# Block-Toeplitz rows of the S5 layer: eight shifted matmuls against eight copies within SBUF

## The chip, the cores and the metric

The kernel runs on one core of a Trainium2 chip, in float32 throughout (some matmuls on operands split into two fp32r parts). The metric is the device time of one launch, in microseconds.

## The reference, cut to what matters

Two blocks of two layers each are applied to x of 512 tokens by 1024 channels. The change touches the first layer of the first block alone, in its state-space half: an S5 layer with 32 groups of 16 channels, each group with 64 complex states.

```python
bu_re = jnp.einsum('blgp,gnp->blgn', ug, bb_re)
bu_im = jnp.einsum('blgp,gnp->blgn', ug, bb_im)
_, _, x_re, x_im = lax.associative_scan(_complex_affine_combine, (a_seq_re, a_seq_im, bu_re, bu_im), axis=1)
y = jnp.einsum('blgn,gpn->blgp', x_re, c_re) - jnp.einsum('blgn,gpn->blgp', x_im, c_im)
```

Everything else (the mLSTM half of that layer, two gated feed-forward parts, an HGRN2 layer, two attention layers with spatial gating and two convolved feed-forward parts) is computed by code that the diff leaves alone.

## The kernel before, in words

Each engine has its own hand-written program (`@block.sync`, `gpsimd`, `tensor`, `scalar`, `vector`), which runs in the order written; semaphores are the only links. Weights come in slabs of 128 by 1024 numbers through a ring of four: SyncE loads `w_raw`, ScalarE copies it to `w_hi` (L1336, `split`), VectorE subtracts to get `w_lo` (L1849), TensorE multiplies each slab in three terms (`product`, L673, 24 matmuls of 512 columns per slab).

The first layer begins with `project()`: twelve slabs of the input projection, with the preparation of the S5 layer laid between them. The sequence of 512 steps is cut into 64 blocks of STEP = 8. For each group g the kernel needs three 128 by 128 matrices: `s5_in` (8 inputs of 16 channels to the 128 state rows), `s5_out` (state rows to 8 outputs of 16 channels), and `s5_conv`, the block-Toeplitz matrix that maps the 8 inputs of a block directly to its 8 outputs. Row block k of a column block j of `s5_conv` is the kernel matrix for a lag, and is zero where the lag is negative. All lags of all groups stand once in `s5_k` (128 partitions, 32 groups by 16 columns, a view of the tile `sq_sum`): TensorE computes it in line 851 (32 small matmuls, 64 passes), ScalarE copies it from PSUM in line 1434. `s5_conv[:, :, j]` is `s5_k` shifted down by 16·(7 − j) partitions. Before the change this shift is a matmul with a shifted identity (`shifted`, L859, eight of them, one for each j), into PSUM banks 5 to 7 in turn, and ScalarE copies each bank to SBUF (L1449). TensorE does this between the last two pairs of slabs; ScalarE between `gate_in(1)` and `gate_in(2)`.

In the meantime VectorE runs a long list of its own: the powers for `s5_q` and `s5_out`, a wait for ScalarE (L2112), cosine and sine tables by doubling (L2125 to L2153), two `w_lo` slabs, a few small operations on `lb_raw` with an exponential by ScalarE in their middle (L1454). GpSimd issues the DMAs that store `us` to DRAM (L619) and load it again by step into `u_step` (L624, eight DMAs of 128 KB); it waits next for the result `ys_step` (L625).

`s5_core()` follows on TensorE. `enter(i)` (L871, 16 passes each) forms the states' inputs for 8 groups; ScalarE copies them to `s5_state` (L1471, behind the exponential of L1454 on its queue); `swap_inputs(i)` (L878) exchanges halves; VectorE turns and scans (`turn_and_sum`, L2184). When all four quarters are scanned, TensorE does `swap_sums` (L882), VectorE `turn_back`, and TensorE `leave(i)`: for each of 32 groups one matmul with `s5_conv[:, g]` as the stationary operand on 64 columns of `u_step` (L889), and one with `s5_out[:, g]` on 63 columns of the state (L891). An fp32 matmul shows as two passes in the profile, each with a weight load of 128 columns. ScalarE copies the outputs (L1475), GpSimd stores and reloads them (L628 to L631), and TensorE goes on with `lstm_front()` (L914 and after).

Of the kernel before, what the change touches and what calls it, by code (L numbers as in the profile page):

```python
# [18 lines left out]
ACT = mybir.ActivationFunctionType  # L19
AX = mybir.AxisListType  # L20

P = 128
# [36 lines left out]
STEP = 8  # L59
# [92 lines left out]
def program(nc, a):  # L152
    ctx = ExitStack()
    with ctx:
# [11 lines left out]
        def sem(name):  # L166
            return ctx.enter_context(nc.semaphore(name))
# [64 lines left out]
        s5_out = m("s5_out", [P, GROUPS, STEP, GW], 40)  # L232
        s5_conv = m("s5_conv", [P, GROUPS, STEP, GW], 56)
        s5_cos = m("s5_cos", [P, GROUPS, CH], 72)
# [6 lines left out]
        s5_cx = m("s5_cx", [P, GROUPS, GW], 84)  # L241
        s5_k = sq_sum[:].rearrange("p (g w) -> p g w", g=GROUPS)
        s5_flat = tmp[:, 2:4].rearrange("p t n -> p (t n)")
# [123 lines left out]

        prep, hgrn = signals("prep"), signals("hgrn")
        s5 = {k: sem(f"s5_{k}") for k in ("pe_to_vector", "pe_to_scalar", "vector_to_pe", "scalar_to_pe")}

# [196 lines left out]
        def _(pool):  # L567
# [54 lines left out]
            for i in range(STEP):  # L622
                k = STEP - 1 - i
                pool.dma_start(u_step[GW * k:GW * k + GW], by_step[i]).then_inc(us_loaded, 16)  # L624
            pool.wait_ge(ys_ready, 1)  # L625
            by_step = ys_dram.rearrange("(g p) j c -> j p g c", p=GW)
# [23 lines left out]
        def _(pe):  # L650
# [173 lines left out]
            def project():  # L824
# [29 lines left out]
                product(h_hi, h_lo, [KD], 2)  # L854
                pe.wait_ge(prep["scalar_to_pe"], n(prep["scalar_to_pe"]))
                for j in range(STEP):
                    out = take(5 + j % 3)
                    off = P - GW * (STEP - 1 - j)
                    nc.tensor.matmul(out[:], shifted[:, off:off + P], s5_k.rearrange("p g w -> p (g w)"),  # L859
                                     start=True, stop=True).then_inc(prep["pe_to_scalar"], 1)  # L860
                product(h_hi, h_lo, [KD], 2)

            def s5_core():
# [20 lines left out]
                def leave(i):  # L884
                    out = take(i)
                    pe.wait_ge(s5["vector_to_pe"], n(s5["vector_to_pe"]))
                    for g in range(8):
                        c = g * CH
                        nc.tensor.matmul(out[:, c:c + CH], s5_conv[:, 8 * i + g].rearrange("p j w -> p (j w)"),  # L889
                                         u_step[:, 8 * i + g], start=True, stop=False)  # L890
                        mm = nc.tensor.matmul(out[:, c + 1:c + CH], s5_out[:, 8 * i + g].rearrange("p j w -> p (j w)"),  # L891
                                              s5_state[:, 8 * i + g, 0:CH - 1], start=False, stop=True)
                    mm.then_inc(s5["pe_to_scalar"], 1)

                pe.wait_ge(us_loaded, 16 * STEP)
                enter(0)
                enter(1)
# [429 lines left out]
        def _(act):  # L1327
# [74 lines left out]
            def project():  # L1402
# [26 lines left out]
                for i in range(GROUPS // 4):  # L1429
# [4 lines left out]
                nc.scalar.activation(s5_k, bank[4][:].rearrange("p (g w) -> p g w", g=GROUPS), ACT.Copy)\  # L1434
                    .then_inc(prep["scalar_to_pe"], 1)
                act.drain().then_inc(bank_free[4], 1)
# [8 lines left out]
                for t in (0, 1):  # L1445
                    gate_in(t)
                for j in range(STEP):
                    act.wait_ge(prep["pe_to_scalar"], n(prep["pe_to_scalar"]))
                    nc.scalar.activation(s5_conv[:, :, j], bank[5 + j % 3][:].rearrange("p (g w) -> p g w", g=GROUPS),  # L1449
                                         ACT.Copy).then_inc(bank_free[5 + j % 3], 1)  # L1450
                for t in (2, 3):
# [1442 lines left out]
```

## Time and profile before

| | us |
|---|---|
| median of 3 runs | 2513.64 (2512.18 to 2513.93) |
| the profiled execution | 2510.49 |
| its span, first to last instruction | 2508.7 |

| engine | busy us | share of the span |
|---|---|---|
| TensorE matmul | 2397.1 | 96% |
| TensorE weight load | 1948.0 | 78% |
| VectorE | 1478.1 | 59% |
| ScalarE | 1078.2 | 43% |
| GpSimd | 160.4 | 6% |

The span is what the profiler sees; 1.8 us of the execution lie around it. TensorE's matmuls are pipelined, so that successive ones overlap in the records: the distance from one start to the next tells the cost, and the sum of the durations is larger. The granted clock is given as a share of full speed: 1.00 is 2.4 GHz, 0.50 is 1.2 GHz. All that the change touches lies in the first 175 us of the span.

### The profile page before, as it was taken

What the parts mean: (1) busy time and instruction counts of PE and PEld (TensorE: products, weight loads), DVE (VectorE), ACT (ScalarE), POOL (GpSimd) and SP (SyncE); (2) the same over time, 40 slices, a digit from 0 to 9 for tenths busy, and PEclk for the clock granted to TensorE, in tenths of its full rate; (3) what the DMA queues carried; (4) which work ended last, traced back from release to release, by engine and by line L of the source; (5) the groups of instructions that cost most, each with busy time, mean ns of one, the idle gap of its engine ahead of it and who ended that gap; (6) DMA issues with size and microseconds to landing.
All of it is one profiled execution on the core that took longest, in us unless ns stands there. A gap on an engine that the chain in (4) does not pass through costs nothing.

```text
span 2508.7 us, 33052 instructions
## 1 busy us (share of the span) xinstructions
PE 2397.1 (96%) x11563; PEld 1948.0 (78%) x11563; DVE 1478.1 (59%) x2157; ACT 1078.2 (43%) x1454; POOL 160.4 (6%) x159
## 2 busy tenths in 40 slices
PE   8987999999989999999999999999999989999999
PEld 6755788888778877888887667788888767788887
DVE  7985464442567745545324776887633686687732
ACT  5344543332456544333324562545422473454421
POOL 2010200000100001000002021000011011000000
PEclk9998999999999999999999999999999999999999
DMA  7320233333222222333333202333333201233331
GB/s 171 84 62 23 76 109 100 92 92 97 71 76 75 75 64 71 103 97 90 100 96 99 68 1 68 99 102 92 94 98 102 84 24 51 84 100 100 88 100 63
DMA packets 400950, 209.65 MB, mean 84 GB/s; under 512 B 18131, under 2 KB 397655, under 8 KB 400871
## 3 DMA queue, kind: packets, MB, share of 16 engines
q1 hardware_dynamic: 397111, 199.65, 27.8%
q0 software_dynamic: 3424, 8.91, 1.4%
q8 instruction: 49, 0.80, 0.1%
q14 instruction: 30, 0.25, 0.0%
q10 hardware_dynamic: 336, 0.05, 0.0%
HBM read 204.38 MB, written 4.19 MB: 83 GB/s over the span
## 4 chain that ended last, share of the span: by engine, by line
PE 84%; DVE 9%; ACT 3%; issue 2%; DVEq 1%; DMA 0%; ACTq 0%; SPq 0%
PE bank L673 66%; PE bank L709 4%; PE bank L1262 2%; PE bank L713 2%; DVE w_lo L1849 1%; DVEq L1878 1%; DVE small L2645 1%; PE bank L988 1%; ACT w_hi L1336 1%; PE bank L1238 1%; DVE tmp L1881 1%; PE bank L1213 1%; PE bank L1134 0%; PE bank L739 0%; PE bank L1092 0%
## 5 line engine op out<-in xcount | busy, mean ns | idle before, releaser
L1849 DVE TENSOR_TENSOR w_lo<-w_raw,w_hi 128x1024 fp32r<-128x1024 f32 x380 | 475.0, 1251 | 630.4 <-ACT w_hi L1336 625.4
L673 PE MATMUL bank<-h_hi,w_hi 128*128 128x512 f32 x1840 | 727.2, 395 | 4.2 <-DVEq L1878 3.9
L673 PE MATMUL bank<-h_lo,w_hi 128*128 128x512 f32 x1840 | 717.5, 390 | 0.0
L673 PE MATMUL bank<-h_hi,w_lo 128*128 128x512 f32 x1840 | 717.3, 390 | 0.0
L1336 ACT ACTIVATE w_hi<-w_raw 128x1024 fp32r<-128x1024 f32 x380 | 401.6, 1058 | 668.4 <-PE bank L673 651.3
L673 PEld LDWEIGHTS bank<-h_hi,w_hi 128*128 128x128 f32 x1840 | 346.5, 188 | 79.8 <-issue 8.1
L673 PEld LDWEIGHTS bank<-h_hi,w_lo 128*128 128x128 f32 x1840 | 346.5, 188 | 73.3 <-issue 2.9
L673 PEld LDWEIGHTS bank<-h_lo,w_hi 128*128 128x128 f32 x1840 | 346.1, 188 | 73.3
L673 PE MATMUL bank<-hid_hi,w_hi 128*128 128x512 f32 x704 | 273.9, 389 | 0.0
L673 PE MATMUL bank<-hid_hi,w_lo 128*128 128x512 f32 x704 | 273.9, 389 | 0.0
L673 PE MATMUL bank<-hid_lo,w_hi 128*128 128x512 f32 x704 | 273.9, 389 | 0.0
L673 PEld LDWEIGHTS bank<-hid_hi,w_lo 128*128 128x128 f32 x704 | 132.2, 188 | 27.6
L673 PEld LDWEIGHTS bank<-hid_hi,w_hi 128*128 128x128 f32 x704 | 132.2, 188 | 27.4
L673 PEld LDWEIGHTS bank<-hid_lo,w_hi 128*128 128x128 f32 x704 | 132.2, 188 | 27.2
L1336 ACT ACT_TABLE_LOAD x44 | 56.5, 1283 | 120.6 <-PE bank L673 120.2
L1790 ACT ACTIVATE tmp<-bank,par 128x512 f32<-128x512 f32 x88 | 68.0, 772 | 85.4 <-DVE bank L2797 85.4
L1881 DVE TENSOR_TENSOR tmp<-tmp 128x512 f32<-128x512 f32 (+3 forms) x122 | 75.0, 623 | 26.7 <-DVE tmp L1881 13.5
L709 PE MATMUL bank<-h_hi,w_hi 128*128 128x512 f32 x168 | 71.5, 425 | 16.0 <-ACT h_hi L1597 9.9
L2797 DVE TENSOR_TENSOR bank<-bank,sq_sum 128x512 f32<-128x512 f32 x88 | 61.6, 700 | 31.8 <-PE bank L673 16.3
L2804 DVE SCALAR_TENSOR_TENSOR tmp<-bank,par,tmp 128x511 f32<-128x511 f32 x88 | 66.0, 750 | 12.0 <-DVE tmp L1890 3.1
L709 PE MATMUL bank<-h_hi,w_lo 128*128 128x512 f32 x168 | 69.7, 415 | 0.0
L1890 DVE SCALAR_TENSOR_TENSOR tmp<-bank,par,tmp 128x511 f32<-128x511 f32 x88 | 65.8, 747 | 2.8 <-ACT tmp L1790 2.3
(462 smaller groups left out, 2856.2 us busy)
## 6 DMA issues: line engine op xcount, KB each, us to landing
w_raw<-in_ffn_w SPq DMA_DIRECT2D x120, 512.0 KB, 3.8
w_raw<-in_w_up SPq DMA_DIRECT2D x88, 512.0 KB, 3.8
w_raw<-in_c_w_in SPq DMA_DIRECT2D x32, 512.0 KB, 4.1
w_raw<-in_w_down SPq DMA_DIRECT2D x32, 512.0 KB, 3.9
w_raw<-in_w_in SPq DMA_DIRECT2D x28, 512.0 KB, 3.9
w_raw<-in_w_o SPq DMA_DIRECT2D x16, 512.0 KB, 3.9
w_raw<-in_ab_w_in SPq DMA_DIRECT2D x12, 512.0 KB, 6.2
w_raw<-in_ffn_w SPq DMA_DIRECT2D x16, 384.0 KB, 3.4
```

Source lines behind the costliest of these rows:

```text
L673: mm = nc.tensor.matmul(out[:], w[:, s, k], v[:, kt], start=(kt == 0 and w is w_hi and v is hi), stop=(kt == sum(slabs) - 1 and v is lo))
L709: nc.tensor.matmul(out[:], w[:, s, k], hi[:, k], start=(first and w is w_hi), stop=False)
L713: mm = nc.tensor.matmul(out[:], w_hi[:, s, k], lo[:, k], start=False, stop=last)
L988: mm = nc.tensor.matmul(bank[b][:], w[:, b, k], v[:, k], start=(first and w is w_hi and v is h_hi), stop=(last and v is h_lo))
L1262: mm = nc.tensor.matmul(out[:], w[:, s, k0 + k], v[:, k], start=(k == 0 and w is w_hi and v is hi), stop=(k == 3 and v is lo))
L1336: nc.scalar.activation(w_hi[:, s], w_raw[:, s], ACT.Copy).then_inc(hi_done, 1)
L1790: nc.scalar.activation(tmp[:, 2 * p + v], bank[(first + 2 * p + v) % RING][:], ACT.Identity, scale=col_at("up_conv", k + 2 * KF), bias=col ...
L1849: nc.vector.tensor_tensor(w_lo[:, s], w_raw[:, s], w_hi[:, s].bitcast(F32), ALU.subtract).then_inc(lo_done, 1)
L1881: step(nc.vector.tensor_tensor(out, x0, x1, op))
L1890: step(nc.vector.scalar_tensor_tensor(out, x0, sc, x1, op0, op1))
L2797: own(nc.vector.tensor_tensor(bank[b][:], bank[b][:], inv_all, ALU.mult), bank_scaled)
L2804: ins = nc.vector.scalar_tensor_tensor(c_[:, 0:SEQ - 1], bank[b][:, 1:SEQ], col_at("up_conv", k + 4 * KF), c_[:, 0:SEQ - 1], ALU.mult, ALU ...
```

## The change

The eight shifted matmuls and their eight copies out of PSUM are taken away. `s5_k` is written with the group as its innermost index, (w g) in place of (g w), so that each partition's 512 numbers can be moved as one run. GpSimd, once it has issued the loads of `u_step`, waits for `s5_k` (`s5_k_ready`) and issues eight DMAs within SBUF: copy j moves partitions 0 to 127 − r of `sq_sum` to partitions r to 127 of `s5_conv[:, j]`, with r = 16·(7 − j). Seven memsets on GpSimd write zeros to the partitions above. `s5_conv` has the layout [P, STEP, GW, GROUPS], so that the stationary operand of a group is read with a distance of 32 numbers (128 bytes) between neighbours. TensorE waits for all eight copies and all seven memsets before `enter(0)`.

```diff
-        s5_conv = m("s5_conv", [P, GROUPS, STEP, GW], 56)
+        s5_conv = m("s5_conv", [P, STEP, GW, GROUPS], 56)
...
-        s5_k = sq_sum[:].rearrange("p (g w) -> p g w", g=GROUPS)
+        s5_k = sq_sum[:].rearrange("p (w g) -> p g w", g=GROUPS)
...
                 pool.dma_start(u_step[GW * k:GW * k + GW], by_step[i]).then_inc(us_loaded, 16)
+            pool.wait_ge(s5_k_ready, 1)
+            for j in range(STEP):
+                r = GW * (STEP - 1 - j)
+                pool.dma_start(s5_conv[r:P, j].rearrange("p w g -> p (w g)"), sq_sum[0:P - r]).then_inc(s5_conv_in, 16)
+            for j in range(STEP - 1):
+                nc.gpsimd.memset(s5_conv[0:GW * (STEP - 1 - j), j], 0.0).then_inc(s5_conv_zero, 1)
             pool.wait_ge(ys_ready, 1)
...
                 product(h_hi, h_lo, [KD], 2)
-                pe.wait_ge(prep["scalar_to_pe"], n(prep["scalar_to_pe"]))
-                for j in range(STEP):
-                    out = take(5 + j % 3)
-                    off = P - GW * (STEP - 1 - j)
-                    nc.tensor.matmul(out[:], shifted[:, off:off + P], s5_k.rearrange("p g w -> p (g w)"),
-                                     start=True, stop=True).then_inc(prep["pe_to_scalar"], 1)
                 product(h_hi, h_lo, [KD], 2)
...
-                        nc.tensor.matmul(out[:, c:c + CH], s5_conv[:, 8 * i + g].rearrange("p j w -> p (j w)"),
+                        nc.tensor.matmul(out[:, c:c + CH], s5_conv[:].rearrange("p j w g -> p (j w) g")[:, :, 8 * i + g],
                                          u_step[:, 8 * i + g], start=True, stop=False)
...
                 pe.wait_ge(us_loaded, 16 * STEP)
+                pe.wait_ge(s5_conv_in, 16 * STEP)
+                pe.wait_ge(s5_conv_zero, STEP - 1)
                 enter(0)
...
-                    .then_inc(prep["scalar_to_pe"], 1)
+                    .then_inc(s5_k_ready, 1)
...
-                for j in range(STEP):
-                    act.wait_ge(prep["pe_to_scalar"], n(prep["pe_to_scalar"]))
-                    nc.scalar.activation(s5_conv[:, :, j], bank[5 + j % 3][:].rearrange("p (g w) -> p g w", g=GROUPS),
-                                         ACT.Copy).then_inc(bank_free[5 + j % 3], 1)
```

GpSimd's queue between the loads of `u_step` and the stores of `ys_step`. Before:

```order
L624 DMA u_step<-us_dram 16x32x64 x8
L628 DMA ys_dram<-ys_step 16x32x64 x8
L629 DMA us<-us_dram 128x4x512
```

With the change (line numbers from here on are later by seven on this queue):

```order
L625 DMA u_step<-us_dram 16x32x64 x8
L629 DMA s_conv<-sq_sum 16x512
L629 DMA s_conv<-sq_sum 32x512
L629 DMA s_conv<-sq_sum 48x512
L629 DMA s_conv<-sq_sum 64x512
L629 DMA s_conv<-sq_sum 80x512
L629 DMA s_conv<-sq_sum 96x512
L629 DMA s_conv<-sq_sum 112x512
L629 DMA s_conv<-sq_sum 128x512
L631 MEMSET s_conv 112x512
L631 MEMSET s_conv 96x512
L631 MEMSET s_conv 80x512
```

Four more memsets, of 64, 48, 32 and 16 partitions, follow, and then the stores of `ys_step`: fifteen instructions stand in a place where there were none.

ScalarE's queue from the copy of `s5_k` (the tile `sq_sum`) on. Before:

```order
L1434 ACTIVATE sq_sum<-bank 128x512
L1336 ACTIVATE w_hi<-w_raw 128x1024
L1443 ACT_TABLE_LOAD
L1443 ACTIVATE zs<-bank 128x512
L1336 ACTIVATE w_hi<-w_raw 128x1024
L1443 ACTIVATE zs<-bank 128x512
L1449 ACTIVATE s_conv<-bank 128x32x16 x8
L1336 ACTIVATE w_hi<-w_raw 128x1024
```

With the change:

```order
L1437 ACTIVATE sq_sum<-bank 128x32x16
L1339 ACTIVATE w_hi<-w_raw 128x1024
L1446 ACT_TABLE_LOAD
L1446 ACTIVATE zs<-bank 128x512
L1339 ACTIVATE w_hi<-w_raw 128x1024
L1446 ACTIVATE zs<-bank 128x512
L1339 ACTIVATE w_hi<-w_raw 128x1024
```

The eight copies are gone and nothing takes their place; the order of the rest is the same, as it is on TensorE's and VectorE's queues.

## Rows read from the trace of the kernel before

**Rows 1.** Chain that ended last, 84 to 176 us: start, us, what.

```profile
110.90 1.30 DVE s_sin L1887
...
115.14 0.59 ACT s_state L1471
...
138.29 0.22 PE bank L891 x2
```

**Rows 2.** Timeline of VectorE, 84 to 136 us: start, us, instruction, [idle before <-releaser].

```profile
84.19 0.62 DVE L1881 TENSOR_TENSOR s_v<-s_v 128x32 f32<-128x32 f32 x4
...
112.22 2.36 DVE L1849 TENSOR_TENSOR w_lo<-w_raw,w_hi 128x1024 fp32r<-128x1024 f32 x2
...
115.27 0.17 DVE L1881 TENSOR_TENSOR small<-small 128x8 f32<-128x8 f32 x1 [0.33 <-ACT small L1454]
...
117.07 0.69 DVE L1881 TENSOR_TENSOR s_w<-bank,s_sin 128x512 f32<-128x512 f32 x1 [0.44 <-PE bank L878]
...
135.22 0.69 DVE L1881 TENSOR_TENSOR s_w<-bank,s_sin 128x512 f32<-128x512 f32 x1 [2.28 <-PE bank L882]
```

**Rows 3.** Timeline of TensorE's matmuls, 92 to 172 us.

```profile
93.58 7.03 PE L859 MATMUL bank<-sq_sum,lead 128*128 128x512 f32 x16
100.05 0.80 PE L673 MATMUL bank<-h_hi,w_hi 128*128 128x512 f32 x1
...
111.37 3.68 PE L871 MATMUL bank<-u_step,s_in 128*128 128x64 f32 x32
115.87 1.10 PE L878 MATMUL bank<-s_state,early 128*128 128x512 f32 x2 [0.82 <-ACT s_state L1471]
...
133.03 5.09 PE L882 MATMUL bank<-s_z,early 128*128 128x512 f32 x8 [9.82 <-DVEq L1878]
137.96 0.33 PE L889 MATMUL bank<-u_step,s_conv 128*128 128x64 f32 x2
...
152.28 3.65 PE L914 MATMUL bank<-xm,s_v 128*64 128x512 f32 x8
```

**Rows 4.** Timeline of ScalarE, 76 to 130 us.

```profile
81.01 0.60 ACT L1434 ACTIVATE sq_sum<-bank 128x512 f32<-128x512 f32 x1 [7.44 <-PE bank L851]
...
115.02 0.22 ACT L1454 ACTIVATE small<-small 128x16 f32<-128x16 f32 x1 [0.61 <-DVEq L1878]
```

**Rows 5.** Groups of weight loads: busy us, mean ns | idle before.

```profile
L889 PEld LDWEIGHTS bank<-u_step,s_conv 128*128 128x128 f32 x64 | 9.7, 192 | 0.5 <-issue 0.5
L891 PEld LDWEIGHTS bank<-s_state,s_out 128*128 128x128 f32 x64 | 9.7, 192 | 0.0
```

**Rows 6.** Groups of VectorE instructions by shape.

```profile
L2277 DVE TENSOR_TENSOR gated_ys<-ys,gate 128x512 f32<-128x512 f32 x4 | 4.4, 1105 | 3.8 <-ACTq L1518 3.8
...
L2283 DVE TENSOR_TENSOR h_lo<-gated_ys,h_hi 128x512 fp32r<-128x512 f32 x4 | 2.7, 686 | 0.3
...
L2619 DVE TENSOR_REDUCE small<-prob_t 128x8 f32<-128x512 f32 x8 | 4.9, 680 | 3.5 <-ACTq L1711 3.5
...
L2216 DVE TENSOR_REDUCE small<-tmp 128x96 f32<-128x384 f32 x1 | 0.8, 828 | 0.0
```

**Rows 7.** Stretches, of line 851 alone: PE, PEld busy (count), clock, DMA.

```profile
76.00:77.00 1.00, 1.00 (x11) 1.00 (x10) 1.00 0.30 37
79.00:80.00 1.00, 1.00 (x7) 1.00 (x6) 0.50 1.28 225
```

**Rows 8.** Stretches: PE, PEld, DVE, ACT, POOL busy (count), clock, DMA.

```profile
125.00:126.00 1.00, 0.00 (x0) 0.00 (x0) 0.90 (x2) 0.00 (x0) 0.00 (x0) 0.81 0.00 0
135.00:136.00 1.00, 1.00 (x3) 0.48 (x2) 0.79 (x2) 0.00 (x0) 0.00 (x0) 0.57 0.00 0
```

**Rows 9.** GpSimd's timeline, then DMA issues: KB each, median us to landing.

```profile
75.38 5.04 POOL L624 DMA_DIRECT2D u_step<-us_dram  x8 [4.79 <-DMA us_dram<-us]
...
u_step<-us_dram POOLq DMA_DIRECT2D x8, 128.0 KB, 5.8
```

**Rows 10.** Timeline of VectorE while GpSimd adds squares.

```profile
257.79 1.72 DVE L1849 TENSOR_TENSOR w_lo<-w_raw,w_hi 128x1024 fp32r<-128x1024 f32 x1 [0.52 <-ACT w_hi L1336]
```

More of the change, by code:

```diff
@@ L368, in program @@
         prep, hgrn = signals("prep"), signals("hgrn")
+        s5_k_ready, s5_conv_in, s5_conv_zero = (sem(k) for k in ("s5_k_ready", "s5_conv_in", "s5_conv_zero"))
         s5 = {k: sem(f"s5_{k}") for k in ("pe_to_vector", "pe_to_scalar", "vector_to_pe", "scalar_to_pe")}
```

## The prediction

> **What bounds the kernel now.** I read the chain that ended last first, in the stretch of the change. From 84 to 114.5 us it names VectorE alone, the tables of lines 2125 to 2153 and then `w_lo` [rows 1]. It passes through ScalarE's copy of the states' input at 115.14, through VectorE's scans up to 133, and from there through TensorE: `swap_sums`, then L889 and L891 in turn. So TensorE is busy at 93 us without holding anything up. The other views say the same. VectorE's timeline has no idle bracket after 84.19, where it passes its wait for ScalarE (L2112), until 115.27, where it waits 0.33 us for an exponential, and 117.07, where it waits 0.44 us for `swap_inputs(0)` [rows 2]. TensorE ends `enter(1)` at 115.05 (111.37 and 3.68) and waits until 115.87 for ScalarE; it waits 9.82 us more before L882 [rows 3]. ScalarE could not have copied the states' input earlier, because the exponential ahead of it on its queue began at 115.02 and waited for VectorE itself [rows 4]. After 133 the picture turns: TensorE runs from 137.96 to 152.28 through `leave` without a gap, and `lstm_front` begins right behind it.
>
> **What goes.** The eight shifted matmuls hold TensorE from 93.58 to 100.05, 6.47 us [rows 3]. All of it lies beside VectorE's list. Nothing in that list waits for it: the `w_hi` slabs that come 6.5 us earlier (the third at about 99.6, the fourth at 105) feed the two `w_lo` at 112.22, which VectorE reaches only then, without idling [rows 2]. TensorE ends `enter(1)` at 108.6 in place of 115.05 and waits for the same copy at 115.14. Gain: 0. ScalarE's eight copies go too; its queue had room there, gain 0. What is late next is VectorE's list, which the change doesn't shorten.
>
> **What the earlier end costs.** TensorE's pause before `swap_inputs(0)` grows from 0.82 to about 7.3 us. The pause before L882 shows what such a pause does: the matmul before it ended at 123.2 (133.03 less 9.82), the granted clock fell during 125 to 126 (mean 0.81, then 0.50), and it was still at 1.2 GHz when work came back, up to 135.9 (mean 0.57 in the slice) [rows 3, 8]. There VectorE could begin 2.19 us after the first matmul's start (135.22 against 133.03); behind L878, at 2.4 GHz, 1.20 us (117.07 against 115.87) [rows 2, 3]. I take the difference, +1.0 us (0 if the clock stays up; the two passes of L878 take 1.10 us at 2.4 GHz, so 1.1 more at most). It lands on VectorE's chain. The later quarters are covered: TensorE is done with them at 123.2, VectorE's part lasts until 133.
>
> **The copies.** GpSimd is through with `u_step` at 80.42 and `s5_k` is written at 81.61 [rows 9, 4]. Its eight issues took 5.04 us, so eight more end at about 86.7; with 5.8 us to landing (the median of the `u_step` DMAs) the last lands at about 92.5. Together they move 576 partition rows of 2 KB, 1.2 MB, somewhat more than the 1 MB of `u_step`. TensorE asks for them at about 105, and would lose nothing until 111.4, where `enter(0)` starts today. Cost 0; the cover is 12 us, and without it each microsecond beyond 111.4 is one on the path. The memsets follow the issues. GpSimd's adds of 512 columns are the nearest rows: one beside `w_lo` stretched it to 1.72 us against 1.18 (2.36 for two) [rows 10, 2]. If each of seven memsets did the same to VectorE, whose list is the path here, that would be 3.5 us; they read nothing and the instructions beside them are short, so I take 0, and keep 0 to +3.5. The Trainium skill (SBUF — State Buffer, Who interferes with whom and the two separate sides) says that a VectorE operation on two SBUF inputs is blocked only by a GpSimd operation that reads SBUF; by that rule the memsets cost nothing here.
>
> **`s5_k` written with a distance of 128 bytes.** It took 0.60 us [rows 4]; at 1.8 times (below) it ends 0.5 us later, at 82.1. VectorE asks at 84.19 and GpSimd has 12 us. Cost 0.
>
> **The stationary operand read with a distance of 128 bytes.** This is the term that decides. `leave` runs 128 passes in 14.32 us, 112 ns each [rows 3], and the loads fill that time: those of L889 and L891 have 192 ns each and 0.5 and 0.0 us idle [rows 5]. A load that takes longer is paid in full, 64 times. No row shows a weight load with a distance. The nearest rows are VectorE's with 32 bytes between neighbours. `gated_ys`, written so, takes 1105 ns, where the like operation on the same tile without it takes 686. The sum over `tmp`, read so, takes 828 ns for 384 numbers, where L2619 takes 680 for 512 in a row [rows 6]. Less some 170 ns that even 8 columns take [rows 2], that is 1.83 against 1.01 ns, and 1.71 against 1.00 ns for each number. As a factor (1.7) on 112 ns: 78 ns more, 5.0 us. As a time for each number (1.83 by 128 columns, 234 ns): 122 ns more, 7.8 us. I take half speed, 224 ns, between the two: 64 · 0.112 = +7.2 us. The lower end is 0, as TensorE is another engine. The Trainium skill speaks on both sides. SBUF — State Buffer, Door 1: The DMA port swizzle, says that SBUF is read in lines of 16 bytes and that an fp32 access is free of cost up to a distance of 4, so 32 pays; VectorE's rows agree. TensorE: Matmul & The Clock Gate, LDWEIGHTS, gives the load's time by the number of columns alone, 107 ns for 128 (the 112 ns here agree), and by that the term is 0 and the sum +1.0.
>
> **Sum.** 0 + 1.0 + 0 + 7.2 = +8.2 us. Everything after `leave` hangs on its end, `lstm_front` directly and the way of `ys_step` through DRAM too, so it arrives whole. The profiled execution would take 2518.7 in place of 2510.49; that execution is 3.15 us under the median of the runs, so I put the sum on the median: 2521.8. A measurement of this kernel can tell about 0.2%, 5.0 us, from no change.
>
> **Rivals.**
> 1. *The strided load costs nothing* (chance 0.27). The loads keep 112 ns, and the pause's +1.0 is all: 2514.6, no change. For it: the load works through columns at a pace of its own, 0.88 ns each, and no row shows TensorE slowed by a layout. Against it: rows 6. It decides at 63 ns more for each load, 175 ns: below that the change stays within 5.0 us.
> 2. *Slower loads thin the matmuls and the clock falls in `leave`* (0.12). Line 851 shows it: matmuls of 16 columns behind full weight loads; in 76 to 77 clock 1.00 and 11 passes, in 79 to 80 clock 0.50 and 7 passes [rows 7]. If `leave` fell so a quarter of the way through (I guess the place), its other 16.1 us would take 11/7 as long, 9.2 us more, and `lstm_front` would start slow, some 1.4 more (half of 133.03 to 135.9): 8.2 + 10.6 = +18.8, 2532.4. Against it: L889's matmuls have 64 columns, L851's 16.
> 3. *GpSimd or the copies come late* (0.04): memsets that block VectorE, or copies landing after 111.4; with the forecast's loads up to 2525.3.
> 4. *TensorE sets the start of the core after all* (0.04): the 6.47 us come through and the loads are free, 2507.2, faster. Rows 2 speak against it.
>
> That the change doesn't do what it says has no chance of its own: the queues show the copies in and the matmuls out, and both layouts are plain in the code.
>
> **The numbers.** The forecast has 0.53; its own range is 5.0 + 0 to 7.8 + 1.1, 2518.6 to 2522.5, and 2526 with the memsets' bound. The range takes in rival 1 with the runs' scatter of about 1 us each way, and goes part of the way to rival 2: 2512.5 to 2529. Slower 0.53 + 0.12 + 0.03 = 0.68, same 0.27 + 0.01 = 0.28, faster 0.04.
>
> **What would show it.** TensorE busy to 108.6 and then idle to about 115.9; clock 0.50 around 115.9 and VectorE's first turn at about 118.1 in place of 117.07; `leave` 21.5 us long in place of 14.3, with L889's loads about twice as long and L891's unchanged; the copies landed by 95. Wrong it would be if `leave` stayed at 14.3, if its clock fell, if TensorE stood at the copies' semaphore, or if VectorE's list from 84 to 114.5 changed in length.

## The result and the profile after

| | before | after |
|---|---|---|
| median of 4 runs, us | 2512.91 (2510.12 to 2513.93) | 2530.28 (2529.18 to 2531.36) |
| ratio, 95% interval | | 1.0070 [1.0058, 1.0082] |
| the profiled execution, us | 2510.49 | 2530.91 |
| its span, us, and mean granted clock | 2508.7, 0.979 | 2529.1, 0.970 |

The change makes the kernel slower by 17.4 us, where the forecast said 8.2: slower, as forecast, but more than twice as much, and 1.3 us above the range. Lines after the edit have moved: L851, L871, L878, L882, L889, L891 and L914 of before are L858, L872, L879, L883, L890, L892 and L917 here.

The chain that ended last shows a first loss where the forecast had none. It runs through VectorE's list as before [rows 1], but one operation of 128 by 32 numbers stands in it with 3.37 us:

```profile
89.00 3.37 DVE s_v L1884
```

VectorE's timeline gives the same operation, and then the turns of the four quarters, which stood at 117.07, 121.08, 125.10 and 129.12 before:

```profile
84.64 0.62 DVE L1880 TENSOR_TENSOR s_v<-s_v 128x32 f32<-128x32 f32 x4 [0.95 <-ACTq L1440]
...
88.91 3.44 DVE L1884 TENSOR_SCALAR s_v<-s_v 128x32 f32<-128x32 f32 x1
...
118.97 0.17 DVE L1880 TENSOR_TENSOR small<-small 128x8 f32<-128x8 f32 x1 [0.33 <-ACT small L1453]
...
121.72 0.69 DVE L1880 TENSOR_TENSOR s_w<-bank,s_sin 128x512 f32<-128x512 f32 x1 [1.38 <-PE bank L879]
...
126.84 0.69 DVE L1880 TENSOR_TENSOR s_w<-bank,s_sin 128x512 f32<-128x512 f32 x1 [1.31 <-PE bank L879]
...
131.96 0.69 DVE L1880 TENSOR_TENSOR s_w<-bank,s_sin 128x512 f32<-128x512 f32 x1 [1.30 <-PE bank L879]
...
135.98 0.69 DVE L1880 TENSOR_TENSOR s_w<-bank,s_sin 128x512 f32<-128x512 f32 x1 [0.20 <-DVE s_z L2183]
```

The reader is to see three things. VectorE waited at 84.64 for ScalarE (0.95 us, none before) and went on 0.45 us later than before (84.19). The TENSOR_SCALAR at 88.91 took 3.44 us; its like at 85.18, 85.93 and 86.68 took 0.17. So the operation behind the exponential stands at 118.97 and not at 115.27 [rows 2], 3.70 us later. And the turns are 5.12, 5.12 and 4.02 us apart where they were 4.02 each time, so that the offset grows from 4.65 at the first turn to 6.86 at the last two.

GpSimd's timeline puts its seven memsets exactly under the slow operation, 88.99 to 92.31; ScalarE's shows the strided write of `s5_k`, 1.07 us against 0.60 [rows 4]:

```profile
84.79 4.21 POOL L629 DMA_DIRECT2D s_conv<-sq_sum  x8 [4.83 <-ACT sq_sum L1437]
88.99 3.32 POOL L631 MEMSET s_conv<- 112x512 f32 x7
```

```profile
83.43 1.07 ACT L1437 ACTIVATE sq_sum<-bank 128x512 f32<-128x512 f32 x1 [10.25 <-PE bank L858]
```

Before comparing stages, one difference has to be set aside, since it lies ahead of the change. `s5_k` was copied 2.42 us later here (83.43 against 81.01), although nothing in front of it was edited: the clock fell to 0.50 during the computation of `s5_k` from about 74 us on, and before from about 78 us on. In the profiled executions of all twelve kernels that copy begins anywhere from 80.65 to 83.43. What hangs on this moment is scatter and not the change.

TensorE's timeline (start, us, instruction, [idle before <-releaser]), to be read beside rows 3:

```profile
107.33 3.68 PE L872 MATMUL bank<-u_step,s_in 128*128 128x64 f32 x32
119.57 2.04 PE L879 MATMUL bank<-s_state,early 128*128 128x512 f32 x2 [8.56 <-ACT s_state L1470]
...
139.89 6.73 PE L883 MATMUL bank<-s_z,early 128*128 128x512 f32 x8 [6.86 <-DVEq L1877]
146.46 0.43 PE L890 MATMUL bank<-u_step,s_conv 128*128 128x64 f32 x2
...
146.95 0.59 PE L890 MATMUL bank<-u_step,s_conv 128*128 128x64 f32 x2
147.38 0.39 PE L892 MATMUL bank<-s_state,s_out 128*128 128x63 f32 x2
147.60 0.59 PE L890 MATMUL bank<-u_step,s_conv 128*128 128x64 f32 x2
...
152.83 0.64 PE L890 MATMUL bank<-u_step,s_conv 128*128 128x64 f32 x2
153.27 0.64 PE L892 MATMUL bank<-s_state,s_out 128*128 128x63 f32 x2
153.69 0.64 PE L890 MATMUL bank<-u_step,s_conv 128*128 128x64 f32 x2
...
171.75 6.11 PE L917 MATMUL bank<-xm,s_v 128*64 128x512 f32 x8
177.79 3.84 PE L921 MATMUL bank<-lstm_bd,xm 128*128 128x128 f32 x32
```

`enter(1)` ended at 111.0 (107.33 and 3.68) and the pause before `swap_inputs(0)` was 8.56 us. `leave` begins at 146.46 and `lstm_front` at 171.75: 25.3 us in place of 14.32. Early in `leave` a pair of passes of L890 takes 0.43 us (146.95 to 147.38) and one of L892 0.22; late in it both take 0.43. The stretches of TensorE (busy (count), clock, DMA share, GB/s) say why the second half of that is so:

```profile
120.00:125.00 5.00, 5.00 (x19) 0.50 0.44 129
125.00:130.00 5.00, 5.00 (x19) 0.50 0.00 0
145.00:150.00 5.00, 5.00 (x26) 0.90 0.00 0
150.00:155.00 5.00, 5.00 (x30) 0.78 0.01 3
155.00:160.00 5.00, 5.00 (x25) 0.50 0.00 0
```

The clock was 0.50 from 120 to 130, at a time when TensorE worked without a gap, was mostly back in 145 to 150, and fell again during 150 to 155, though TensorE had not stood still. The mean loads of the two lines, both 192 ns in rows 5, mix both clocks:

```profile
L890 PEld LDWEIGHTS bank<-u_step,s_conv 128*128 128x128 f32 x64 | 17.2, 317 | 0.7 <-issue 0.5
L892 PEld LDWEIGHTS bank<-s_state,s_out 128*128 128x128 f32 x64 | 14.8, 284 | 0.0
```

Summed as offsets of the two profiled executions: 3.70 at the exponential, 0.95 more at the first turn, 2.21 more at the fourth, 1.64 more in the phase of L883 (6.57 us from its first start to `leave`, 4.93 before), 10.97 in `leave`, 2.46 in the first eight passes of `lstm_front` (171.75 to 177.79, 6.04 us, against 3.58). That is 21.93. Of it 1.5 is lost again further on, since the kernel before has the clock at 0.50 from 188 to 193 and the changed one at the same work does not until 211; 20.4 is left, the difference of the spans.

### The profile page after: what moved, and what is told of

Its sections match the earlier page's. It is cut to its first block, busy times and chain, and to the rows that moved or that the text cites. A ratio compares the mean times of both kernels' runs of the same rounds, so it can differ in the third digit from the quotient of the medians.

```text
span 2529.1 us, 33034 instructions
## 1 busy us (share of the span) xinstructions
PE 2413.1 (95%) x11547; PEld 1964.0 (78%) x11547; DVE 1481.5 (59%) x2157; ACT 1073.8 (42%) x1446; POOL 167.9 (7%) x174
## 4 chain that ended last, share of the span: by engine, by line
PE 86%; DVE 7%; ACT 3%; issue 2%; DVEq 1%; DMA 0%; ACTq 0%; SPq 0%
PE bank L680 67%; PE bank L716 4%; PE bank L1265 2%; PE bank L720 2%; DVE w_lo L1848 1%; DVEq L1877 1%; DVE small L2644 1%; PE bank L991 1%; ACT w_hi L1339 1%; PE bank L1241 1%; PE bank L1216 1%; PE bank L890 1%; DVE tmp L1880 1%; PE bank L1137 0%; PE bank L892 0%
```

## The experiments

The theory behind the first four: the loss has three independent parts, the strided read (with the clock in `leave`), the memsets that hold VectorE, and TensorE's pause. Each kernel was compared with the kernel before on its own chip. The offsets of the profiled executions against the profiled one of before are collected here, in us; the ratios are of all runs.

| kernel | exponential (ScalarE) | 4th turn | start of `leave` | length of `leave` | second line of `lstm_front` | ratio [95%] |
|---|---|---|---|---|---|---|
| changed | +3.70 | +6.86 | +8.50 | 25.3 | +21.93 | 1.0070 [1.0058, 1.0082] |
| e1, strided layouts alone | +2.11 | +2.10 | +2.69 | 25.7 | +15.80 | 1.0051 [1.0034, 1.0068] |
| e2, consecutive read | +3.19 | +6.34 | +7.90 | 14.3 | +7.91 | 1.0016 [1.0006, 1.0026] |
| e3, zeros by ScalarE | +2.12 | +5.28 | +6.96 | 25.3 | +20.41 | 1.0069 [1.0052, 1.0086] |
| e4, idle matmuls kept | +2.04 | +3.63 | +3.90 | 25.7 | +16.87 | 1.0068 [1.0051, 1.0085] |
| e6, zeros behind the flag | −0.31 | +2.84 | +4.42 | 25.3 | +17.83 | 1.0057 [1.0040, 1.0074] |
| e7, all three undone | 0.00 | −0.01 | +1.57 | 14.3 | +1.58 | 1.0006 [0.9994, 1.0018] |
| e8, copies in pieces | −0.17 | +0.77 | +2.31 | 14.3 | +2.32 | 1.0000 [0.9987, 1.0012] |
| e9, e6 and pause filled | −0.89 | −0.34 | −0.05 | 25.7 | +12.91 | 1.0033 [1.0019, 1.0046] |
| e10, e8 and pauses filled | +1.17 | +3.01 | +2.79 | 14.4 | +2.87 | 1.0007 [0.9996, 1.0017] |

The ratios, times 2513 us, lie up to 4.6 us under the last offsets (e4 and e7 agree with theirs): some 1.5 us is the part lost again further on, and the profiled execution of before was 2.4 us under its median. The rest is scatter; an interval is 2.5 to 4.3 us to each side, so a term of a microsecond is read from the profiles and only the large ones from the medians as well. Absolute times of different chips are not compared: the medians of the kernel before lie between 2511.36 and 2516.30 on those used here.

### e1: the strided layouts alone

```diff
 (against the kernel before)
-        s5_conv = m("s5_conv", [P, GROUPS, STEP, GW], 56)
+        s5_conv = m("s5_conv", [P, STEP, GW, GROUPS], 56)
-        s5_k = sq_sum[:].rearrange("p (g w) -> p g w", g=GROUPS)
+        s5_k = sq_sum[:].rearrange("p (w g) -> p g w", g=GROUPS)
...
-                        nc.tensor.matmul(out[:, c:c + CH], s5_conv[:, 8 * i + g].rearrange("p j w -> p (j w)"),
+                        nc.tensor.matmul(out[:, c:c + CH], s5_conv[:].rearrange("p j w g -> p (j w) g")[:, :, 8 * i + g],
```

> The kernel before with the new layouts alone: the eight shifted matmuls and ScalarE's copies stay, s5_k and s5_conv have the group innermost, so the stationary operand in leave() is read with a distance of 128 bytes. No copies by DMA, no memsets, no longer pause ahead of swap_inputs(0). Theory (the strided loads are slow by themselves, about 215 ns against 112, and make the clock fall in leave): leave() takes 21 us at first and, after some 6 us, 213 ns for each pass, 25 us in all; lstm_front starts slow; 11 to 13.5 us over the kernel before, 2524 to 2527. Rival 1 (the clock falls in leave only because of the pause before it): leave() 20.9 us at clock 1.00, 6.6 us over before, 2519.5. Rival 2 (the loads are slow only at the lower clock): no change, 2513.

Measured: 2523.67 us (2523.15 to 2524.94), 1.0051, +12.8. TensorE's timeline:

```profile
140.65 0.43 PE L889 MATMUL bank<-u_step,s_conv 128*128 128x64 f32 x2
...
166.34 5.39 PE L914 MATMUL bank<-xm,s_v 128*64 128x512 f32 x8
171.66 3.84 PE L918 MATMUL bank<-lstm_bd,xm 128*128 128x128 f32 x32
```

`leave` takes 25.7 us here too, and `lstm_front` starts slow (5.32 us to L918, against 3.58), although TensorE had no pause ahead of `swap_inputs` and VectorE's turns were 4.0 us apart. So the strided read alone lengthens `leave` by 11 us and lowers the clock in it, as the theory said (the time is 0.3 us under its range); with neither 20.9 us nor 14.3, both rivals fall. The 2.1 us at the exponential are two waits: 0.77 us for `s5_k` at 84.40, and 1.74 us for the fourth `w_hi` at 115.36. Both come from a TensorE that was late: it released `s5_k` at 83.17, 2.16 us later than before (the scatter named above), the copy of the fourth `w_hi` began 2.72 us later (114.28 against 111.56), and with the eight shifted matmuls still in TensorE's queue that lateness reached VectorE. So the eight matmuls had been off the path by about one microsecond (2.72 less 1.74).

### e2: the layouts and copies stay, the read is consecutive

```diff
-                        nc.tensor.matmul(out[:, c:c + CH], s5_conv[:].rearrange("p j w g -> p (j w) g")[:, :, 8 * i + g],
+                        nc.tensor.matmul(out[:, c:c + CH], s5_conv[:].rearrange("p j w g -> p (j w g)")[:, P * (8 * i + g):P * (8 * i + g) + P],
```

> The changed kernel, but leave() reads 128 consecutive numbers of s5_conv in place of 128 with a distance of 32, so it multiplies by numbers of the wrong places: the matrix of the state-space half is not the Toeplitz matrix, the rest is as in the changed kernel. Theory: loads of 112 ns again and leave() at 14.3 us and clock 1.00; what is left over the kernel before is the memsets' hold on VectorE (3.3), the copy of s5_k (0.5) and the clock after the pause (0.9 to 4.8): 2517 to 2521. Rival 1 (the pause makes the clock fall in leave): leave() near 25 us although the loads are consecutive, 2528 or more.

Measured: 2515.38 us (2513.04 to 2516.97), 1.0016, +4.0; less than expected.

```profile
145.86 0.33 PE L890 MATMUL bank<-u_step,s_conv 128*128 128x64 f32 x2
...
160.19 3.65 PE L917 MATMUL bank<-xm,s_v 128*64 128x512 f32 x8
```

`leave` is back at 14.33 us, so rival 1 falls, and up to its start all is as in the changed kernel but for 0.6 us. By the medians what is not the strided read costs about 4 us, then (1.5 to 6.5), and the read itself 13 to 14; by the profiles it is 7.9 and 14.0.

### e3: the zeros by ScalarE, ahead of the flag

```diff
-            for j in range(STEP - 1):
-                nc.gpsimd.memset(s5_conv[0:GW * (STEP - 1 - j), j], 0.0).then_inc(s5_conv_zero, 1)
...
                     .then_inc(s5_k_ready, 1)
+                for j in range(STEP - 1):
+                    r = GW * (STEP - 1 - j)
+                    nc.scalar.activation(s5_conv[0:r, j], lead[0:r, 0:1].unsqueeze(2).to_broadcast([r, GW, GROUPS]), ACT.Copy)\
+                        .then_inc(s5_conv_zero, 1)
```

> The changed kernel with the seven memsets moved from GpSimd to ScalarE (copies of a zero, behind the copy of s5_k, where ScalarE is idle for 6.8 us). Theory (a VectorE tensor_scalar was held for as long as GpSimd's memsets ran): the 3.44 us operation of VectorE goes back to 0.17 and the list ends 3.3 us earlier, 2527. Rival 2 (GpSimd's DMA issues or the copies themselves held VectorE): the long operation stays, now beside the issues, and the time stays at 2530. Rival 3 (ScalarE's zeros delay its next w_hi or VectorE's wait for it): up to 4 us are given back.

Measured: 2528.61 us (2527.67 to 2529.40), 1.0069. VectorE's timeline:

```profile
86.19 0.62 DVE L1882 TENSOR_TENSOR s_v<-s_v 128x32 f32<-128x32 f32 x4 [2.60 <-ACTq L1442]
86.73 0.30 DVE L1886 TENSOR_SCALAR s_v<-s_v 128x32 f32<-128x32 f32 x1
```

The slow operation is gone, but the seven copies (3.73 us) stand on ScalarE's queue ahead of the flag that VectorE waits for, and the wait of 2.60 us takes back about half of it: the exponential is 1.58 us ahead of the changed kernel's. Rival 2 falls, since GpSimd's issues are all there, and rival 3 came. The edit traded one hold for another; e6 repeats it in a better place.

### e4: eight unread matmuls where the shifted ones were

```diff
                 product(h_hi, h_lo, [KD], 2)
+                pe.wait_ge(bank_free[5], n.now(bank_free[5]) + 1)
+                for j in range(STEP):
+                    nc.tensor.matmul(bank[5][:], ident, x[:, 0], start=True, stop=True)
                 product(h_hi, h_lo, [KD], 2)
```

> The changed kernel with eight matmuls of the old size between the last two pairs of slabs, whose results nobody reads: TensorE ends enter(1) as late as before, and pauses under 4 us ahead of swap_inputs(0) (the rest of the pause is the hold on VectorE). Theory (the pause lowers the clock for the whole of s5_core): with the shorter pause swap_inputs and enter run at 2.4 GHz, VectorE's later turns no longer wait for TensorE, 2 to 5 us less than the changed kernel, 2525 to 2528; leave() still falls. Rival (3.7 us of pause are enough to lower it): no difference, 2530.

Measured: 2528.14 us (2527.99 to 2528.39), 1.0068. The pause is 2.09 us long, `swap_inputs(0)` runs at 2.4 GHz, and yet the clock falls right behind it (0.50 from 120 to 130) and the turns are 4.50, 5.12 and 4.02 apart. Here 0.5 and 1.1 us came onto VectorE's chain. VectorE's TENSOR_SCALAR was held for 2.87 us, to the end of the memsets; the TENSOR_TENSOR ahead of it overlapped the first 0.5 us of them and took its usual time. In the profile `leave` starts 4.6 us earlier than in the changed kernel, as the theory had it, but the medians (1.0068 and 1.0070) show none of that; with 4.3 us of interval to each side they don't decide.

### e5: a table of weight loads

```diff
                     mm.then_inc(out_turned, 1)
+            x_row = x[:].rearrange("p k n -> p (k n)")
...
+            for _ in range(16):
+                nc.tensor.matmul(bank[0][:, 0:64], x_row[:, 0:1017:8], x_row[:, 0:64], start=True, stop=True)
```

> The kernel before with a table of matmuls appended after its last step: for distances 1, 2, 3, 4, 5, 8, 16 and 32 between the numbers of the stationary operand, sixteen matmuls of 64 columns each; then, behind 48 matmuls of 512 columns each time, 128 thin matmuls at distance 1 and 64 at distance 32. The appended work is extra and its total time says nothing. Theory (the load is slow where neighbouring numbers lie in different 16-byte lines, and the slow loads alone lower the clock): a matmul takes about 112 ns at distances 1 to 3, 215 ns at 4 and beyond, no more at 32 than at 8; the clock falls to 1.2 GHz within the 64 strided matmuls (13.8 us at 215 ns) and stays at 2.4 GHz within the 128 consecutive ones (14.3 us at 112 ns). Rival A (it grows with the distance): times between 112 and 215 ns at 2 to 16. Rival B (the clock falls because the matmuls are thin, and distance only adds time): the 128 consecutive ones lose the clock too.

The groups of weight loads (busy us, mean ns | idle before), one line for each of the distances 1, 2, 3, 4, 5, 8, 16 and 32, each from a stretch at clock 1.00:

```profile
L1331 PEld LDWEIGHTS bank<-x 128*128 128x128 f32 x20 | 2.3, 192 | 0.0
...
L1335 PEld LDWEIGHTS bank<-x 128*128 128x128 f32 x19 | 2.3, 196 | 0.0
...
L1339 PEld LDWEIGHTS bank<-x 128*128 128x128 f32 x15 | 2.7, 260 | 0.2 <-issue 0.2
...
L1343 PEld LDWEIGHTS bank<-x 128*128 128x128 f32 x19 | 4.5, 329 | 0.0
...
L1347 PEld LDWEIGHTS bank<-x 128*128 128x128 f32 x24 | 5.4, 317 | 0.1
...
L1351 PEld LDWEIGHTS bank<-x 128*128 128x128 f32 x18 | 4.4, 334 | 0.1
...
L1355 PEld LDWEIGHTS bank<-x 128*128 128x128 f32 x22 | 4.9, 311 | 0.1
...
L1359 PEld LDWEIGHTS bank<-x 128*128 128x128 f32 x20 | 4.4, 310 | 0.0
```

A load's record grows from 192 ns (distance 1) and 196 (2) to 260 (3), 329 (4), 317 (5), 334 (8), 311 (16) and 310 (32). These records overlap; from start to start it is 110 ns a pass at distance 1 (24 us for 218, below) and 212 at 32 (6.77 us for 32). The theory held but for distance 3, where half of the rise is there already (68 of the 137 ns at distance 4), and rival A fell: nothing is added beyond 4. Then the long stretches: 128 thin matmuls at distance 1, and 64 at distance 32 shortly after their start and later (busy (count) of the engines, clock):

```profile
2652.00:2676.00 24.00, 24.00 (x218) 24.00 (x217) 0.00 (x0) 0.00 (x0) 0.00 (x0) 1.00 0.01 1
2720.50:2723.00 2.50, 2.50 (x13) 2.50 (x13) 0.00 (x0) 0.00 (x0) 0.00 (x0) 1.00 0.00 0
2728.00:2745.00 17.00, 17.00 (x80) 17.00 (x80) 0.00 (x0) 0.00 (x0) 0.00 (x0) 0.50 0.00 1
```

For 28.5 us (2650.47 to 2679.00) consecutive thin matmuls kept the clock at 1.00. The strided ones lost it within 4 us (mean 0.67 in 2722 to 2726), with TensorE busy all the time, and it fell in or behind the short groups of distances 3 to 32 as well. Rival B falls: it is the strided load, not the 64 columns alone, that lowers the clock. And 17 us for 80 passes at 1.2 GHz is 213 ns each, as at 2.4 GHz: the strided pass pays nothing for the low clock.

### e6: the zeros by ScalarE, behind the flag

```diff
                 act.drain().then_inc(prep["scalar_to_vector"], 1)
+                for j in range(STEP - 1):
+                    r = GW * (STEP - 1 - j)
+                    nc.scalar.activation(s5_conv[0:r, j], lead[0:r, 0:1].unsqueeze(2).to_broadcast([r, GW, GROUPS]), ACT.Copy)\
+                        .then_inc(s5_conv_zero, 1)
                 act.wait_ge(prep["vector_to_scalar"], n(prep["vector_to_scalar"]))
```

(and the memsets of GpSimd away, as in e3)

> The changed kernel with the seven memsets written by ScalarE instead of GpSimd, and behind the flag that lets VectorE go on, so that nobody waits for them. Theory (the memsets on GpSimd hold one VectorE instruction for 3.3 us on the path): the TENSOR_SCALAR of L1884 takes 0.17 to 0.3 us, VectorE's exp comes at about 115.7 us instead of 119.0, and the kernel takes 2525 to 2527.5 us, 3.3 us less than the changed kernel and up to 2 more if the shorter pause keeps the clock. Rival (any other writer into the same rows holds VectorE, or the time is lost elsewhere): 2529 to 2531 us.

Measured: 2527.26 us (2526.15 to 2529.22), 1.0057. VectorE's timeline:

```profile
88.17 0.17 DVE L1886 TENSOR_SCALAR s_v<-s_v 128x32 f32<-128x32 f32 x1
...
117.71 0.69 DVE L1882 TENSOR_TENSOR s_w<-bank,s_sin 128x512 f32<-128x512 f32 x1 [1.39 <-PE bank L877]
...
122.83 0.69 DVE L1882 TENSOR_TENSOR s_w<-bank,s_sin 128x512 f32<-128x512 f32 x1 [1.32 <-PE bank L877]
```

The exponential is at 114.71, 4.0 us ahead of the changed kernel's; the place that took 3.44 us takes 0.17. `leave` starts 4.1 us earlier. Of that 3.3 are the memsets, 0.3 lies upstream, and 0.45 is the wait for `s5_k`, which is not there although ScalarE's write is still strided (81.05 and 1.10 us, done before VectorE asks): in the changed kernel the matmuls ahead of that copy had ended 2.4 us later. The turns are still 5.12, 5.12 and 4.01 apart, after a pause of 7.75 us. The medians agree within their intervals: 17.6 less 14.3 us.

### e7: all three undone

The edits of e2, e6 and e4 together.

> The changed kernel with a consecutive stationary read (128 consecutive numbers, wrong places, so the output is not the reference's), the zeros by ScalarE behind the flag, and eight unread 512-column matmuls in the place of the eight shifted ones. Theory (the three costs found make up the whole difference): the kernel is back within 1.5 us of the kernel before, 2511.5 to 2514 us, with 0.5 us left for the strided write of s5_k. Rival (something not yet named costs as well, the copies by DMA for example): 2515 us or more.

Measured: 2515.61 us against 2516.30 of before on the same chip, ratio 1.0006 [0.9994, 1.0018]. The expectation's bounds were absolute (2511.5 to 2514, the rival from 2515 up) and don't fit a chip on which the kernel before takes 2516.30; the ratio speaks for the theory. The turns stand at 117.07, 121.08, 125.10 and 129.11, to 0.01 us those of before. Nothing that was not named costs anything that can be seen: the eight copies by DMA are free. The phase of L883 takes 6.50 us here as well, so the 1.64 us counted for it above is not the change's but the clock's (0.50 up to 138 here; 0.57 in 135 to 136 before [rows 8]), which rose at 135.9 in the one and not before 138 in the other.

### e8: copies in pieces of 64 bytes

```diff
+        s5_conv = m("s5_conv", [P, GROUPS, STEP, GW], 56)
+        s5_k = sq_sum[:].rearrange("p (g w) -> p g w", g=GROUPS)
...
+                pool.dma_start(s5_conv[r:P, :, j], s5_k[0:P - r]).then_inc(s5_conv_in, 16)
...
+                        nc.tensor.matmul(out[:, c:c + CH], s5_conv[:, 8 * i + g].rearrange("p j w -> p (j w)"),
```

Both layouts are those of before, the copy does the rearranging, and the zeros are written as in e6.

> Both layouts as in the kernel before, the eight shifted matmuls replaced by copies that place pieces of 64 bytes (16 numbers) instead of whole rows, the zeros by ScalarE behind the flag: a correct kernel without any strided read or write. Theory: if the copies (28,672 or fewer pieces in 16 engines) land before leave starts at 138 us, only the clock term of the pause is left, 2512 to 2514.5 us. Rival: the pieces land after that and TensorE waits for them at its first matmul of enter, since the wait stands ahead of it; each us they are late past 115 us is a us more, so 2520 us and above if they need 45 us or more.

Measured: 2515.37 us against 2516.30, ratio 1.0000 [0.9987, 1.0012].

```profile
105.92 3.76 PE L870 MATMUL bank<-u_step,s_in 128*128 128x64 f32 x32 [0.77 <-issue]
115.69 2.05 PE L877 MATMUL bank<-s_state,early 128*128 128x512 f32 x2 [6.01 <-ACT s_state L1472]
...
154.60 3.65 PE L915 MATMUL bank<-xm,s_v 128*64 128x512 f32 x8
```

The last of the copies went out at 99.67 and took 6.2 us to land, and TensorE waited 0.77 us at 105.92, in a stretch that has several us of room. The issues are not free either: three TENSOR_SCALARs beside them took 0.27, 0.52 and 0.52 us instead of 0.17, and VectorE's list from 83.24 to the exponential 31.6 us against 30.8 before (84.19 to 115.02). It doesn't show in the table because that list happened to begin 0.95 us earlier. What is left besides is the pause, 6.01 us. `swap_inputs(0)` took 1.84 us instead of 0.9, and the first turn came 0.95 us later behind the exponential than before (117.85 less 114.85, against 117.07 less 115.02). That is the term of +1.0 by itself. Here the clock had returned by the second quarter, and the turns are 4.01 apart.

### e9: e6 with the pause filled

```diff
                 enter(1)
+                fill(7, 8)
                 swap_inputs(0)
```

`fill(b, many)` issues `many` unread matmuls of 512 columns into bank b.

> The changed kernel with the zeros by ScalarE behind the flag (e6) and eight unread matmuls of 512 columns (7 us at full clock) in TensorE's pause ahead of swap_inputs(0). Theory (the pause costs only through TensorE's clock, and that price is separate from the strided read's): the turns of VectorE stand 4.0 us apart again, the profile's leave starts 2 to 3 us earlier than in e6 and still takes 24 to 26 us, and the kernel takes 2524 to 2525.5 us, about what the strided layouts alone took (2523.7). Rival (the clock is low in leave because it was low before it): leave takes 21 us or less, and the kernel 2520 or below.

Measured: 2522.48 us (2518.78 to 2524.39), 1.0033 [1.0019, 1.0046], 1.5 us below the range that was expected.

```profile
108.68 7.09 PE L897 MATMUL bank<-u_step,lead 128*128 128x512 f32 x16
...
137.91 0.43 PE L888 MATMUL bank<-u_step,s_conv 128*128 128x64 f32 x2
...
163.61 5.23 PE L921 MATMUL bank<-xm,s_v 128*64 128x512 f32 x8
```

The turns are 4.02 apart and `leave` starts at 137.91, where it did before and 4.5 us earlier than in e6 (2 to 3 were expected); it still takes 25.7 us. The rival falls: the clock is lost in `leave` even when the quarters ran at 2.4 GHz. The pause ahead of `swap_sums` lowered it here too, but it does so in every kernel but e10, and those with a consecutive read (e2, e7, e8) keep the clock in `leave`. What is left is the strided read alone: 12.9 us as an offset, 8.3 (4.8 to 11.6) by the ratio; e1 gives 12.8 (8.5 to 17.1) for it with its waits, so 8.5 to 11.6 us agrees with both.

### e10: e8 with both pauses filled

```diff
+                fill(7, 6)
                 swap_inputs(0)
...
                 swap_inputs(3)
+                fill(4, 11)
```

> The copies in pieces of 64 bytes (e8) with unread matmuls of 512 columns in TensorE's two pauses: six ahead of swap_inputs(0) and eleven ahead of swap_sums, so that the clock stays at 2.4 GHz. Theory (the clock in swap_inputs and in the 512-column matmuls of swap_sums is all that the pauses cost): the phase of swap_sums takes 3.5 to 4 us instead of 6.6, leave starts 2 to 3 us earlier than in e8, and the kernel is 1 to 3 us faster than the kernel before, at the edge of what can be told. Rival (VectorE's turns bound that stage, so a faster TensorE there is hidden): leave starts less than 1 us earlier, and the kernel takes the time of e8.

Measured: 2514.73 us (2508.62 to 2519.47) against 2513.81, 1.0007 [0.9996, 1.0017].

```profile
136.98 3.60 PE L881 MATMUL bank<-s_z,early 128*128 128x512 f32 x8
140.75 0.41 PE L888 MATMUL bank<-u_step,s_conv 128*128 128x64 f32 x2 [0.17 <-DVE s_state L2203]
```

The phase of `swap_sums` took 3.77 us to `leave` in place of 6.46, as expected; but `leave` waits for VectorE's `turn_back` now (0.17 us at 140.75) and starts 0.48 us later than in e8, since VectorE was 1.3 us later at the exponential (four TENSOR_SCALARs beside the issues took 2.61 us together, 1.48 in e8) and the clock was lost once more in the 2.78 us left of the first pause (second turn at 124.10, 5.12 behind the first). The eleven filling matmuls were also too many: `swap_sums` began 4.85 us behind the fourth turn, and 3.91 before, 0.94 us late. So the theory's earlier `leave` and its 1 to 3 us did not come, and the rival, that VectorE bounds the stage, holds at the end of it; a shorter filling was not tried. No version was faster than the kernel before; e8 equals it.

## Why the prediction was wrong, step by step

Three steps failed: the memsets were put at nothing (3.3 us), the later quarters were called covered (2.2 us), and the clock was taken to stay at 2.4 GHz in and behind `leave` (6.9 us). The term that was to decide, the strided load, was right.

- **What bounds the kernel, and what goes (gain 0): right, with less room than I saw.** VectorE's list sets the start of the core. From the start of that list to the exponential it is 30.9 us with eight 512-column matmuls (e7, 84.11 to 115.02) and 30.9 without (e6, 83.78 to 114.71). But in e1, where TensorE came 2.7 us late at the fourth `w_hi`, they cost 1.74 us, so a gain of that size is there in executions of that kind.
- **The pause, +1.0: the size was right for the first quarter and the sentence "the later quarters are covered" was a step that failed.** The first turn came 0.95 us late in the changed kernel, in e6 and in e8. But the cover holds only at 2.4 GHz. At 1.2 GHz a quarter of `enter` and `swap_inputs` takes TensorE 5.12 us, VectorE's part 4.02, and TensorE becomes the bound: 2 times 1.1 us more (e6, the changed kernel), once (e10), 0.5 and 1.1 (e4), not at all where the clock was back in time (e8) or never fell (e9). I had read the recovery from rows 8, where it came 3 us after work did; here the clock stayed at 0.50 for over 10 us of work without a gap (119.57 to 130).
- **The copies, 0: right.** They were issued from 84.79 to 89.00; e7, which has them all, is at the time of before.
- **The memsets, 0: wrong, and the named bound of +3.5 was near the truth.** They cost 3.3 us. That the bound came so near is luck: it was seven times a stretch of 0.5 us (0.54 by the numbers beside it, 3.8 in all) on operations of `w_lo`, and what happened is one hold for as long as all seven ran. My reason, that they read nothing and the instructions beside them are short, is refuted by the 3.44 us of an instruction of 0.17. The Trainium skill (SBUF — State Buffer, Who interferes with whom) has the rule that fits, beside the one I used: a `tensor_scalar` can run in a mode that takes the port pair shared with GpSimd, and whoever has it blocks the other fully. The trace agrees: the TENSOR_SCALAR was held to the end of the memsets in three kernels (the changed one, e2, e4), and the TENSOR_TENSOR in e4 was not, which is the rule that I had used. That the port is what holds it is the page's account; the runs show the hold, which instruction it strikes, and that it goes with the memsets (e3, e6). I weighed the section for the two-input operations that make up most of the list and not for its nine TENSOR_SCALARs.
- **`s5_k` with a distance, 0: right in size and not safe in cover.** 1.07 to 1.10 us against 0.60, the 1.8 times I took. The cover (2.6 us from 81.61 to 84.19) was enough in e6 and gone in the changed kernel, where the copy itself began 2.42 us later by scatter; 0.45 us came through.
- **The strided stationary operand, +7.2: right for the load, and short by what the clock does.** A pass takes 215 ns where I put 224, so 32 groups cost 6.6 us at full clock. But the clock fell 6.4 us into `leave` (rival 2, to which I gave 0.12). That adds 4.4 us there and 2.5 in `lstm_front`: 10.97 and 2.46, 13.4 in all, beside my 7.2. My reason against the rival, 64 columns are more than 16, fails in e5: consecutive loads with 64 columns keep the clock, strided ones lose it. The rival's size was wrong in another way: I slowed all passes by 11/7, while the strided ones take 213 ns at either clock and only the consecutive ones of L892 double (112 to 213). So rival 2's 2532.4, 2.1 us from the measured time, is near by luck: its clock term is 10.6 where 6.9 was measured, and the memsets and the quarters fill the gap.
- **The two rules on the strided load.** The Trainium skill, SBUF — State Buffer, Door 1: The DMA port swizzle (lines of 16 bytes, fp32 free up to a distance of 4) gave the right side: distance 32 pays. The runs set the edge lower, 260 ns at 3 and 329 at 4 against 192. The Trainium skill, TensorE: Matmul & The Clock Gate, LDWEIGHTS (the time depends on the number of columns alone) holds at 112 ns for consecutive numbers and fails at 215 for these; the measurement decides.

Set beside the forecast of 8.2: memsets 3.3, later quarters 2.2, clock in and behind `leave` 6.9, `s5_k` 0.45, less 0.6 for the load's 215 ns, makes 20.4 at the second line of `lstm_front`; the profile has 21.93 less the 1.64 of L883's phase, 20.3. The medians show 17.4, the rest being what is lost again further on, and scatter. That the memsets, the pause and the read are separate is shown by e6, e9 and e2, each of which takes one away; their sizes to a microsecond rest on one profile each. Two things stay open: why strided loads lower the clock at all, and why it came back within one quarter in e8 and only in the last one in e6, though their pauses were alike (6.0 and 7.8 us).

Not tried: the memsets on GpSimd at a time when VectorE has no TENSOR_SCALAR, and the layout [P, STEP, GROUPS, GW], in which each copy still moves whole rows of an unchanged `s5_k` and a load reads eight runs of 16 consecutive numbers. No run shows what such a load takes.

## What to carry to other kernels

The layout in which a matrix is stored is paid each time it is loaded: an operand read 64 times should be consecutive, and the transfer that is hidden anyway should do the rearranging, even in pieces of 64 bytes (e8). Work taken from an engine that was not the bound bought nothing here and cost its clock, so look at what the engine does at half speed before calling the work behind a pause covered. And work moved to an idle engine must be checked against every kind of instruction beside it; here one instruction was enough.

## What was not expected of the hardware

- A strided weight load lowers TensorE's clock with TensorE busy throughout: lost within 4 us in e5, and 5.0 to 6.4 us into `leave` in the six kernels with a strided read, while 28.5 us of equal consecutive matmuls kept it.
- The load's cost has its whole rise between distances 2 and 4: 192, 196, 260, 329 ns at 1 to 4, then 310 to 334 up to 32. And a strided pass takes 213 ns at 1.2 GHz as at 2.4.
- The moving operand pays as well: in e5 the 16 passes of 512 columns that read at distance 8 (L1361) took 14.8 us (2594.44 to 2609.25), 0.93 each, the first three of them at 1.2 GHz and the rest at 2.4, against 0.43 for the 96 consecutive ones behind them (2609.25 to 2650.47).
- A TENSOR_SCALAR of 128 by 32 numbers, 0.17 us by itself, took 3.44 us beside seven memsets of GpSimd (2.87 in e4; 3.86 in e2, where it began 0.5 us ahead of them, beside the last issue of a copy), and 0.24 to 1.21 us beside GpSimd's issues of the copies in pieces (e8, e10).
